# Experts in steps of 1024 columns instead of 512

## The reference

```python
def moe_swiglu(h, w_router, w_gate, w_up, w_down):
    logits = (h @ w_router).astype(jnp.float32)
    top_val, top_idx = lax.top_k(logits, TOP_K)          # 2 of 8
    ...
    for e in range(N_EXPERTS):
        y = swiglu(h, w_gate[e], w_up[e], w_down[e])      # (silu(h @ g) * (h @ u)) @ d
        out = out + gates[..., e:e + 1].astype(h.dtype) * y
```

## Time and profile before

| | us |
|---|---|
| median of three runs | 1748.35 (1745.25 to 1749.27) |
| the profiled execution | 1750.49 |
| its span, first to last instruction | 1748.8 |

### The profile page before, as it was taken

How to read it: one execution, slowest core, us unless ns; L and a number is a source line. 1 busy time by engine, 2 the same in 40 slices (tenths; PEclk the granted TensorE clock), 3 DMA queues, 4 the chain that set the end, 5 groups by cost and what they waited for, 6 DMA issues and landing times.

```text
span 1748.8 us, 24844 instructions
## 1 busy us (share of the span) xinstructions
PE 1700.8 (97%) x9514; PEld 1457.1 (83%) x9514; DVE 1397.9 (80%) x1202; ACT 1126.4 (64%) x969; POOL 138.1 (8%) x148
## 2 busy tenths in 40 slices
PE   9999999999999998999989999989999899999999
PEld 8889999998888777888768887778887698889998
DVE  7476445656899998889989889998999879868775
ACT  7444443564677777777777778777777655856553
POOL 7100000000110000000000000000000018600000
PEclk9999999999999999999999999999999999999999
DMA  7446564543799999999999999999989944326561
GB/s 258 158 147 217 169 212 162 184 165 121 266 365 382 333 392 389 379 347 349 394 395 372 374 329 378 396 392 380 371 323 394 342 139 145 121 89 208 173 205 49
DMA packets 244655, 479.33 MB, mean 274 GB/s; under 512 B 11791, under 2 KB 80169, under 8 KB 244537
## 3 DMA queue, kind: packets, MB, share of 16 engines
q1 hardware_dynamic: 243673, 476.43, 75.8%
q10 hardware_dynamic: 864, 1.31, 0.2%
HBM read 476.66 MB, written 1.05 MB: 273 GB/s over the span
## 4 chain that ended last, share of the span: by engine, by line
PE 67%; DVE 12%; DMA 10%; issue 4%; ACT 4%; POOL 2%; DVEq 0%; SPq 0%; ACTq 0%; POOLq 0%
PE bank L2213 18%; PE bank L2215 18%; PE bank L2214 18%; DVE wl L1686 7%; DMA arena<-in_moe_w_gate 7%; DMA arena<-in_moe_w_down 3%; ACT wh L1117 2%; PE bank L2332 1%; PE bank L2340 1%; PE bank L2333 1%; PE bank L2669 1%; POOL arena L892 1%; PE bank L2732 1%; POOL arena L891 1%; DVE h L1856 1%
## 5 line engine op out<-in xcount | busy, mean ns | idle before, releaser
L1686 DVE TENSOR_TENSOR wl<-raw,wh 128x2048 fp32r<-128x2048 f32 x224 | 513.4, 2302 | 61.3 <-ACT wh L1117 60.5
L1117 ACT ACTIVATE wh<-raw 128x2048 fp32r<-128x2048 f32 x224 | 429.2, 1918 | 122.7 <-PE bank L2215 74.5
L2213 PE MATMUL bank<-wh,xhl 128*128 128x512 f32 x776 | 309.2, 398 | 7.3 <-DVE wl L1686 6.4
L451 DVE TENSOR_TENSOR wl<-raw,wh 128x2048 fp32r<-128x2048 f32 x112 | 254.9, 2293 | 67.0 <-ACT wh L444 65.3
L2215 PE MATMUL bank<-wh,xhl 128*128 128x512 f32 x776 | 302.9, 390 | 0.0
L2214 PE MATMUL bank<-wl,xhl 128*128 128x512 f32 x776 | 302.3, 390 | 0.0
L2213 PE MATMUL bank<-xhl,wh 128*128 128x256 f32 x944 | 268.0, 284 | 0.2 <-DVE wl L451 0.2
L2215 PE MATMUL bank<-xhl,wl 128*128 128x256 f32 x944 | 267.1, 283 | 0.0
L2214 PE MATMUL bank<-xhl,wh 128*128 128x256 f32 x944 | 267.1, 283 | 0.0
L1686 DVE TENSOR_TENSOR wl<-arena,wh 128x2048 fp32r<-128x2048 f32 x112 | 255.4, 2286 | 6.5 <-ACT wh L1117 6.2
L1117 ACT ACTIVATE wh<-arena 128x2048 fp32r<-128x2048 f32 x112 | 214.4, 1918 | 60.3 <-PE bank L2215 32.2
(11 more groups left out here) (484 smaller groups left out, 2491.4 us busy)
## 6 DMA issues: line engine op xcount, KB each, us to landing
raw<-in_moe_w_up SPq DMA_DIRECT2D x112, 1024.0 KB, 9.0
arena<-in_moe_w_gate SPq DMA_DIRECT2D x96, 1024.0 KB, 8.5
raw<-in_moe_w_down SPq DMA_DIRECT2D x96, 1024.0 KB, 8.0
raw<-in_w_up SPq DMA_DIRECT2D x22, 1024.0 KB, 5.2
raw<-in_moe_w_gate SPq DMA_DIRECT2D x16, 1024.0 KB, 8.5
arena<-in_moe_w_down SPq DMA_DIRECT2D x16, 1024.0 KB, 9.7
raw<-in_gla_w_in SPq DMA_DIRECT2D x12, 1024.0 KB, 7.6
raw<-in_w_in SPq DMA_DIRECT2D x12, 1024.0 KB, 6.6
```

The source lines that it names most:

```text
L451: V.tensor_tensor(wl[:, i % NW, :], raw[:, i % NR, :], wh[:, i % NW, :].bitcast(F32), ALU.subtract).then_inc(lo_of[i][0], 1)
L1117: V.activation(wh[:, s, :], src, ACT.Copy).then_inc(sg("hi_moe"), 1)
L1686: V.tensor_tensor(wl[:, s, :], moe_raw(c)[0], wh[:, s, :].bitcast(F32), ALU.subtract).then_inc(lo_moe, 1)
L2213: T.matmul(o, xh, yh, start=first, stop=False)
```

## The change

Steps become 1024 columns wide, except the last: 1024, 1024, 1024, 512 (four steps instead of seven). A gate or up piece of a wide step is 256 input rows by 1024 columns; it has two runs of 4 KB for each partition, where it had four of 2 KB. Down pieces hold the same 256 rows, but partition p now takes the neighbouring rows 2p and 2p + 1 (8 KB in one run) instead of p and p + 128; the transposes take every second column of `eact` to match. A step has four pieces of each kind, or two in the last. The number of pieces, of bytes and of matmuls stays.

Gate, up and transposes have two banks each (0 and 1, 2 and 3, 4 and 5), the output 6 and 7, and SiLU, product, high copy and residual run over both at once, without a second buffer from step to step. Gate waits for the SiLU, up for the product of the step before. The one-hot matrix moves to bank 5, between two uses by transposes, so the transposes after the third gate wait for its two readers. The hand-written orders at an expert's end stay.

```diff
-    EJ = 512
-    NEJ = FE // EJ
+    STEPS = [(f, min(1024, FE - f)) for f in range(0, FE, 1024)]
+    NEJ = len(STEPS)
...
+        for j, (_, width) in enumerate(STEPS):
+            uorder += [(kind, j, k) for kind in "gu" for k in range(width // 256)]
             if j:
-                uorder += [("d", j - 1, 0), ("d", j - 1, 1)]
+                uorder += [("d", j - 1, k) for k in range(STEPS[j - 1][1] // 256)]
...
-        esg = ar(2 * EJ).rearrange("p (a n) -> p a n", a=2)
-        eact = ar(2 * EJ).rearrange("p (a n) -> p a n", a=2)
+        esg, eact = ar(1024), ar(1024)
...
-                    src = kpn(src)
+                    src = src.rearrange("(p k) n -> p k n", p=P)
                 else:
...
+                    f, width = STEPS[j]
+                    n = PIECE // width * P
+                    src = IN["moe_w_gate" if kind == "g" else "moe_w_up"][0, bass.ds(ee, 1), k * n:(k + 1) * n, f:f + width]
...
-                        if kind == "g" and k == 1:
+                        if kind == "g" and k == LASTK[j]:
...
-                            V.activation(esg[:, n % 2, :], bank[n % 2][:, :], ACT.Silu).then_inc(sg("moe_silu"), 1)
+                            V.activation(esg[:, 0:width], wide(0, width), ACT.Silu).then_inc(sg("moe_silu"), 1)
...
-                            V.tensor_tensor(eact[:, n % 2, :], esg[:, n % 2, :], bank[2 + n % 2][:, :],
+                            V.tensor_tensor(eact[:, 0:width], esg[:, 0:width], wide(2, width),
...
                 def gate(i, j):
 
-                    n = NEJ * i + j
-                    pe.wait_ge(sg("moe_act"), at(2 * NEJ, n + 1))
-                    gate_up(i, bank[n % 2], "g", j)
+                    if not first:
+                        pe.wait_ge(sg("moe_silu"), at(2 * NEJ, NEJ * i + j))
+                    gate_up(i, 0, "g", j)
+
+                def up(i, j):
+
+                    pe.wait_ge(sg("moe_act"), at(2 * NEJ, NEJ * i + j + 1))
+                    gate_up(i, 2, "u", j)
...
-                        for k in range(4):
-                            block_ = eact[:, n % 2, k * P:(k + 1) * P]
+                        for k in range(STEPS[j][1] // P):
+                            rows = eact[:, k // 2 * 256:(k // 2 + 1) * 256].rearrange("p (m two) -> p two m", two=2)[:, k % 2, :]
...
                     def down(j, between=None):
...
-                        for part in range(2):
-                            if part and between is not None:
+                        for part in range(STEPS[j][1] // 256):
+                            if part == 2 and between is not None:
                                 between()
```

More of the change, by code:

```diff
@@ L117, in build @@
         scr = sb("scr", [P, 1])
-        bank = [ctx.enter_context(nc.psum_tensor(f"bank{b}", [P, 512], F32)) for b in range(8)]
+        banks = ctx.enter_context(nc.psum_tensor("bank", [P, 8, 512], F32))
+        bank = [banks[:, b, :] for b in range(8)]
         ar_at = [0]
@@ L2684, in here, with gate_up @@
                     return of(wh, M0 + c, k), of(wl, M0 + c, k)
[L2686 removed]
+                def gate_up(i, b0, kind, j):
                     x = tokens_of(i)
[L2688 to L2699 removed]
+                    width = STEPS[j][1]
+                    rows = PIECE // width
+                    for q in range(KD // rows):
+                        kks = range(rows * q, rows * (q + 1))
+                        halves = [(bank[b0 + a], slice(512 * a, 512 * (a + 1))) for a in range(width // 512)]
+                        if first:
+                            pe.wait_ge(sg("moe_xh"), q // 2 + 1)
+                            h_, l_ = here(UC * i + upos[kind, j, q], rows)
+                            for kk in kks:
+                                for b, ns in halves:
+                                    T.matmul(b, x[:, kk, HIGH], h_[:, kk % rows, ns], start=(kk == 0), stop=False)
+                                    T.matmul(b, x[:, kk, HIGH], l_[:, kk % rows, ns], start=False, stop=False)
+                            pe.wait_ge(sg("moe_xl"), q // 2 + 1)
+                            for kk in kks:
+                                for b, ns in halves:
+                                    ins = T.matmul(b, x[:, kk, LOW], h_[:, kk % rows, ns], start=False, stop=(kk == KD - 1))
                             used(ins)
@@ L2727, in transposed @@
                         n = NEJ * i + j
-                        pe.wait_ge(sg("moe_act"), at(2 * NEJ, n + 3))
-                        for k in range(4):
-                            block_ = eact[:, n % 2, k * P:(k + 1) * P]
+                        pe.wait_ge(sg("moe_act"), at(2 * NEJ, n + 2))
+                        turned = turned_act(i, j)
+                        for k in range(STEPS[j][1] // P):
+                            rows = eact[:, k // 2 * 256:(k // 2 + 1) * 256].rearrange("p (m two) -> p two m", two=2)[:, k % 2, :]
                             if i == 0:
-                                ins = T.transpose(bank[4][:, k * P:(k + 1) * P], block_, ident[:, :])
+                                ins = T.transpose(turned[:, k, :], rows, ident[:, :])
                             else:
-                                ins = T.matmul(bank[4][:, k * CAP[1]:(k + 1) * CAP[1]], block_, fold[:, :], start=True, stop=True)
+                                ins = T.matmul(turned[:, k, :], rows, fold[:, :], start=True, stop=True)
                         ins.then_inc(sg("moe_Tfull"), 1)
@@ L2809, in experts @@
                     pe.wait_ge(sg("moe_yl"), at(4, 2 * i + 1))
-                    scatter(0, 0, bank[7])
+                    scatter(0, 0, bank[5])
                     scatter(1, 0, bank[4])
```

120 lines of the change are left out of this document (56 added, 64 removed).

## The result

The changed kernel takes 1768.93 us (median of 4 runs, 1766.42 to 1770.46) against 1747.66 of the kernel before, timed beside it. The ratio is 1.0121, with an interval of 1.0104 to 1.0139: 21 us slower, outside the range of the forecast. The profiled execution took 1770.46 us with a span of 1768.7; the span before was 1748.8.

The account below looks back on a forecast made before the run. TensorE was taken to bound full experts, VectorE and late transfers light ones. Light experts -3.2, clock +4 and seams 1 made +2 on the profiled 1750.5 us; less 2.1 to the median, 1750.0 us, range 1739 to 1763.

Parts of the forecast that it names:

- hand-over: Between experts, 48 instead of 24 matmuls between scatter halves: TensorE stalls 3.2 us, VectorE 5.4, seven times.
- light expert: Second of an expert pair, up and down in two products: 3.2 us less at the end of the next piece 3.
- full experts: First of each pair, three products, bound by TensorE: each of three hand-overs into one loses 3.2 us.
- The clock: TensorE after stalls into full experts: half of three draw 1.2 GHz at 2.35 us each, about +4 us.
- -10 + 2.5 (waits): VectorE in a light expert: ten us of waits for data and at the expert's end shrink to 2.5 (0 to 5).
- start of piece 4 behind the scatter: VectorE's split of piece 4 after a hand-over into a light expert: 4.8 us later.
- 101.8 us as priced: VectorE's work in a light expert, piece 4 to the next piece 3: splits, products, residuals, additions, copies; 0.45 us less after.
- no cost: ScalarE's SiLU and copies behind a gate step: four pieces of 2.72 us cover the chain in a full expert.
- rival 4: Longer runs don't speed transfers, 2.70 us being due to addresses: four light experts 6 us longer each, about 1774; chance 0.08.
- even: Expert's end: 3.27 us of TensorE idle before the last transposes replaced by some 3 us waiting for the last residual.
- Rival 3: Hand-over pause leaves DMA without lead, light experts DMA-bound: 3.7 us more in each of four, 1760 to 1765; chance 0.30.
- the 1 us for seams: Allowance of 1 us added to the whole sum for seams not counted.

Follow-up runs that it names:

- e1: Changed kernel with the scatter's second half behind two of the next expert's four gate pieces (24 matmuls) instead of all four: 1734.89 us.
- e4: Kernel before with the next expert's first up step also put ahead of the scatter's second half (40 or 48 matmuls between halves), steps of 512 kept: 1781.16 us.
- e9: e3 with the scatter's second half behind three gate pieces (36 matmuls) instead of two: 1742.66 us.
- e2: Changed kernel with VectorE's one-off sorting block six pieces earlier in the first expert: 1767.04 us.
- e5: e3 with every piece in two DMAs, wide gate and up pieces halved by columns (2 KB runs), down pieces by rows (4 KB): 1744.85 us.
- e6: e3 with every piece in two DMAs, all halved by rows, leaving 4 KB runs: 1735.05 us.
- e3: Changed kernel with the edits of e1 and e2 together: 1733.49 us.

## Why the prediction was wrong

**The hand-over was foreseen at its place and size.** Seven gaps of 3.2 us on TensorE were forecast and 3.13 to 3.61 measured; 5.4 us of VectorE's pause, and 4.3 to 6.1 measured. Into a light expert piece 4 was to start 4.8 us later, and it does: 13.66 us behind the first scatter (816.80 to 830.46) instead of 8.82 (804.8 to 813.62), 4.8 more. The experiments e1, e4 and e9 show the hand-over as the cause from three sides. Of the 15.5 us in full experts the gaps are some 9.9 (forecast 9.6).

**The clock was near.** I took half of three stalls with 2.35 us each, 3.5, and wrote +4; the three cost 3.4, 0 and 1.7, together 5.1.

**The step that failed is the light expert**: "-10 + 2.5 (waits)". I forecast -3.2 us for each, -12.8 for four; measured were -0.9 for all four. For the expert of the earlier trace rows the terms read:

| term | forecast | measured |
|---|---|---|
| start of piece 4 behind the scatter | +4.8 | +4.8 |
| from there to the end of the next piece 3, without idle time (101.8 us as priced) | -0.45 | -0.45 taken as priced (busy time in the view: -1.3) |
| waits in that stretch | -7.5 (10 to 2.5) | -5.7 (10.05 to 4.35 against the priced work) |
| the stretch in all | -7.95 | -6.15 (111.85 to 105.70) |
| end of the next piece 3 | -3.2 | -1.3 |

So 4.35 us of waits stayed where I left 2.5. The faster transfers did what they could: before, only 4.7 us of VectorE's idle time in the stretch stood behind a DMA, and 0.45 of it is left. But I credited them with 7.5.

The rest isn't theirs: the "ten" hold idle time at the ends of steps and of the expert, and 1.7 us that the view counts as busy (103.54 against my 101.8): a split behind an idle time counts with its full 2.28 us, one in a row with 2.20, and 19 such places make about 1.5. And the idle time behind ScalarE's copies of the transposes grew with the wider steps. I had set ScalarE's chain at "no cost", with a reason that I gave for a full expert alone; in this light one it holds 2.2 us of the waits for splits and the 0.4 for the copy itself.

Two smaller parts: from scatter to scatter this expert saved 0.9, not 1.3, as the scatter comes 0.4 us later against that piece 3. And I carried the saving of one light expert, the longest of four (113.8 against a mean of 113.1), to all four: the others saved 0.3 and 0.7 us, and one took 1.0 longer. With the wait undone, e1 shows what the wide steps are worth: 4.8 us a light expert, where my terms without the pause make 8.

**What was not foreseen: the first expert, +5.4 us.** I wrote that the transposes after the third gate wait for the readers of the one-hot matrix in bank 5, and gave it no price. The price hangs on an operation that the sum doesn't name: the sorting block of 5.8 us. It was tied to a down piece of the third step and is now tied to one of the first, two splits ahead of the copy for which those transposes wait. e2 removes the gap; in e1, which left the gap (3.27 us) but drew 3.4 us of the slow clock behind it instead of 6.8, the first scatter came 2.4 us earlier than in the changed kernel.

**What held.** 2.56 us for a piece with runs of 4 KB (e5 and e6 show that run length, not addresses, sets it: rival 4 falls). The gap before the last transposes is gone; the "some 3 us" of TensorE waiting for the last residual are 2.12 (at 924.2 us), so "even" was a microsecond off at most. A product over 1024 columns is 1.21 us long with its successor 1.13 behind its start (896.28 and 897.41 in the timeline), as worked out. Strided transposes cost 0.2 us for a full expert: the value taken, 0, was close. Of the signs, VectorE above 95% busy came (102.24 of 105.70 us, 97%); ScalarE's waits for DMAs "mostly gone" did not (17 of 42 pieces, 21 before), but VectorE hardly waits behind them.

**The rivals.** Rival 3 forecast the sign and, by luck in part, nearly the size: 3.7 us more than my sum in each light expert, where 3.0 were measured on average. Its stretch of 107.5 us came out as 105.7, between that and my 103.9, and e9 shows that the lead doesn't cover the pause. But its mechanism, a light expert bound by the DMA from end to end, isn't in the trace: VectorE's waits behind a DMA are 0.45 us of that stretch, and e3, with no pause, has 18 waits of ScalarE for DMAs where this one has 17. The time beyond the forecast is 5.4 (first expert) + 11.9 (light experts) + 1.9 (15.5 in full experts against 9.6 + 4), less the 1 us for seams: 18.2, and 20.1 - 2 is 18.1.

What stays open: what the chain at the ends of steps is worth. Most of VectorE's 3.4 us of waits in the stretch above stand there, and of the 3.8 in that of e3; no run shortens the chain, by moving ScalarE's copy of the next piece ahead of that of the transposes, say.

## What to carry to other kernels

When a step gets larger, look for what was placed between two steps in whole steps: a wait that was covered by one step of work (none or 0.18 us left) became 4.7 us when the step doubled, and it turned 0.8% faster into 1.2% slower. Part a sum of idle time by what it waits for before a faster transfer is credited with it; of 10 us here 4.7 stood behind a DMA. Where a buffer gets a second tenant, follow its readers' queue back past the change, to whatever one-off block stands ahead of them.

## What the runs showed of the hardware

- Rate of 1 MB weight loads by the length of their runs: 379 to 397 GB/s at 2 KB (a piece in 2.71 us), near 408 at 4 KB (2.56), 401 to 444 at 8 KB. With the same bytes in the same number of DMAs, 388 GB/s with runs of 2 KB in gate and up and 404 with 4 KB (e5, e6). The Trainium skill (DMA: Bandwidth & Descriptors, iDMA fabric) has 408.7 for 4 KiB rows, which the trace agrees with.
- The same idle time of 3.13 us on TensorE drew no slow clock at 945 us (1.00) and 3.4 us of 1.2 GHz at 1186 (0.79); 3.61 us at 702 drew 6.9 (0.57), and only 2.09 us at 681 drew 3.4 (0.79). The Trainium skill (TensorE: Matmul & The Clock Gate, Why this matters for your kernels) warns of idle gaps between bursts. The trace agrees at five of the seven hand-overs and not at the two others, and such a gap in a full expert cost between 0 and 3.4 us beyond itself.
- A transpose whose input has a step of 8 bytes takes 281 ns instead of 272, and its weight load 205 instead of 141. The Trainium skill (SBUF — State Buffer, The DMA port swizzle) has two 4-byte words used in a 16-byte line at full rate; the trace shows 3% less for the transpose, and a load 45% longer.
